# Stick-breaking attention laid out with keys on the partitions and its running sums on TensorE, a one-pass mask and maximum in the softmax blocks, and later output weight parts

## The reference, cut to what matters

```python
# dilated mixture: 12 heads, softmax over banded keys, q,k: 64 columns
s = where(valid, q @ k.T * Dh ** -0.5, -inf); m = max(s); p = exp(s - m); den = sum(p)
o = (p / den) @ v;  lse = m + log(den)          # heads are mixed by softmax(lse)

# latent attention: 8 heads, causal softmax, q,k: 96 columns
o = softmax(where(k <= q, s, -inf)) @ v

# stick breaking: 8 heads, q,k: 64 columns
z = q @ k.T * scale;  strict = k < q
log_one_minus = where(strict, log_sigmoid(-z), 0)
after = cumsum(log_one_minus, reverse) - log_one_minus     # sum over the later keys
weights = exp(where(strict, log_sigmoid(z) + after, -inf));  o = weights @ v

merged = gates[0] * (o_a @ wb_a) + gates[1] * (o_b @ wb_b) + gates[2] * (o_c @ wb_c)
x = x + merged @ w_out
```

## Time and profile before

| | |
|---|---|
| median of 3 runs | 5031.83 us (5019.65 to 5035.23) |
| the profiled execution | 5035.78 us, its span 5034.0 us |
| mean granted clock of TensorE | 0.941 of full speed |
| busy | PE 89%, PEld 62%, DVE 44%, ACT 30%, POOL 16% |
| stage C of the first layer | about 3236.6 to 3396 us in the span |
| the same of the second layer | about 4366.3 to 4525.7 us |

### The profile page before, as it was taken

The page is one execution under the profiler, slowest core; times in us unless marked ns, Lnnn a source line. Parts: engine busy times, 40 slices in busy tenths (PEclk is TensorE's granted clock), DMA queues, the critical chain, the costliest instruction groups (busy, mean ns, idle before and its releaser), DMA issues.

```text
span 5034.0 us, 90473 instructions
## 1 busy us (share of the span) xinstructions
PE 4482.8 (89%) x38676; PEld 3131.1 (62%) x38676; DVE 2228.4 (44%) x3897; ACT 1502.9 (30%) x2632; POOL 791.7 (16%) x499
## 2 busy tenths in 40 slices
PE   6899899988998899979998988878999988878999
PEld 3566666666555554464443965656787955656787
DVE  2555555453355542130112457446434357446343
ACT  2343333332222211010001334443332234443232
POOL 0021111110232230000000321233000321233000
PEclk9899999988999999989999999989999998989999
DMA  6100000000111024238998211114221211114221
GB/s 231 64 33 16 8 19 17 5 26 13 42 46 38 34 90 183 99 121 357 407 409 355 91 61 41 66 52 160 101 96 76 81 61 41 69 53 155 101 101 51
DMA packets 86825, 512.06 MB, mean 102 GB/s; under 512 B 10504, under 2 KB 11032, under 8 KB 45848
## 3 DMA queue, kind: packets, MB, share of 16 engines
q1 hardware_dynamic: 86424, 506.28, 26.3%
HBM read 476.85 MB, written 29.38 MB: 101 GB/s over the span
## 4 chain that ended last, share of the span: by engine, by line
PE 71%; DVE 13%; issue 7%; ACT 3%; DMA 3%; PEld 1%; POOL 1%; SPq 0%; PEldq 0%; DVEq 0%; POOLq 0%; ACTq 0%
PE ps L229 68%; PE ps L232 3%; DVE upper L248 2%; DVE upper L240 2%; ACT upper L287 2%; DMA upper<-in_ew 2%; DVE lower L240 2%; DVE upper L264 2%; PEld ps L229 1%; DVE upper L244 1%; DVE upper L256 1%; DVE rounded L240 1%; ACT lower L287 1%; DVE upper L260 0%; POOL upper L3702 0%
## 5 line engine op out<-in xcount | busy, mean ns | idle before, releaser
L229 PE MATMUL ps<-rounded,rounded 128*128 128x512 f32 (+2 forms) x7968 | 1672.4, 369 | 45.9 <-POOL rounded L3237 21.6
L229 PEld LDWEIGHTS ps<-rounded,rounded 128*128 128x128 f32 x7968 | 1345.9, 194 | 307.5 <-issue 36.0
L229 PE MATMUL ps<-lower 128*128 128x512 f32 (+10 forms) x4976 | 1078.0, 393 | 55.4 <-issue 22.8
L229 PE MATMUL ps<-upper 64*64 64x64 f32 (+8 forms) x15584 | 840.6, 260 | 173.0 <-DVE upper L264 38.9
L287 ACT ACTIVATE upper<-ps 128x512 f32<-128x512 f32 (+6 forms) x953 | 440.2, 491 | 1649.7 <-PE ps L229 1229.0
L229 PEld LDWEIGHTS ps<-upper 64*64 64x64 f32 (+4 forms) x15584 | 598.7, 145 | 445.7 <-issue 185.5
L229 PEld LDWEIGHTS ps<-lower 128*128 128x128 f32 (+3 forms) x4976 | 578.1, 184 | 442.9 <-issue 376.9
L229 PE MATMUL ps<-lower,upper 64*64 64x64 f32 (+6 forms) x7248 | 607.8, 304 | 52.1 <-DMA lower<-in_ada 21.3
L2616 POOL TENSOR_TENSOR rounded<-lower,rounded 128x1024 fp32r<-128x1024 f32 (+2 forms) x90 | 273.0, 3035 | 2009.3 <-ACT rounded L287 2009.0
L287 ACT ACTIVATE upper<-upper 128x512 f32<-128x512 f32 (+9 forms) x693 | 342.7, 501 | 648.7 <-DVE upper L260 167.9
L229 PEld LDWEIGHTS ps<-lower,upper 64*64 64x64 f32 (+3 forms) x7248 | 335.0, 143 | 263.1 <-issue 195.1
(11 more groups left out here) (89 smaller groups left out, 2444.5 us busy)
## 6 DMA issues: line engine op xcount, KB each, us to landing
lower<-in_ew SPq DMA_DIRECT2D x140, 1024.0 KB, 10.4
upper<-in_ew SPq DMA_DIRECT2D x52, 1024.0 KB, 12.9
lower<-in_b0f SPq DMA_DIRECT2D x16, 2048.0 KB, 7.5
lower<-in_b1f SPq DMA_DIRECT2D x16, 2048.0 KB, 7.8
upper<-in_ada SPq DMA_DIRECT2D x18, 1024.0 KB, 5.2
lower<-in_wrkv SPq DMA_DIRECT2D x8, 1728.0 KB, 7.1
lower<-in_b0g SPq DMA_DIRECT2D x24, 512.0 KB, 3.8
gad<-upper SPq DMA_DIRECT2D x48, 256.0 KB, 3.7
```

What stands on the lines that cost most here:

```text
L229: return self.e.matmul(out, lhsT, rhs, start=start, stop=stop)
```

## The change

**Softmax.** `stt` and `red` are replaced by one `tensor_tensor_reduce`, which adds the mask to the scores in PSUM, multiplies by minus the scale and keeps the minimum, so that the mask is scaled too; ACT's exp has scale -1. The built program holds two instructions for it. The score bank is free after it. The 48 negations of `softA` become one of 128x48 at meet latent.

**Stick breaking.** A step of the list is now a head, not a head and 128 queries. The scores stand transposed: keys on partitions, one block of columns for each of the 4 key blocks (512, 384, 128 and 256 queries; 1280 columns over three banks). The 1/8 is applied when the queries are copied out of PSUM. The mask is added by a matmul of the identity with a 128x128 constant. The sum over later keys is a matmul: a triangle of -1 for the key block itself, all -1 for later ones, against the value split into a rounded and a remaining part, accumulated in banks of its own head after the scores were copied out. No transposes, no scan and no POOL step remain. Two heads are in flight, three turns apart, and the filler comes at 1.78 steps a turn for 27 turns.

**Output weight parts.** They are made at d = 5, 6 and 7 and after the last.

```diff
+    def low(self, line, out, a, b, scale, least, *event):
+        self.wait_ge(line)
+        self.e.tensor_tensor_reduce(out, a, b, scale, 3e38, ADD, ALU.min, least).then_inc(line.up(*event), 1)
...
+    def heads(z):
+        for _ in range(3 * z):
+            yield None
+        for hh in range(z, 8, 2):
+            for s in (0, None, None, 1, None, 2):
+                yield None if s is None else ("stick", hh, s)
...
-    drain([lane("stick", 32, 5, z) for z in range(6)], filler, 1.4)
+    drain([heads(z) for z in range(2)], filler, 1.78)
...
+BLOCK_AT = (0, 512, 1024, 896)
...
+    def stick(hh, s):
+        team, slot, use = k.lane[hh % 2], hh % 2, ("stick", l, hh)
+        e = slice(64 * slot, 64 * slot + 64)
+        if s == 0:
+            ps = banks.take_at(use, 3 * slot, 3)
+            for j in (0, 1, 3, 2):
+                pe.mm(ps[:, block_cut(j)], b.ck[e, hh // 2, 128 * j:128 * j + 128], b.cq[e, hh // 2, 128 * j:512], j != 3, False)
+                last = pe.mm(ps[:, BLOCK_AT[j]:BLOCK_AT[j] + 128], pe.ident, k.c2["sb"], False, j != 1)
+            last.then_inc(team.pe.up("score", l, hh), 1)
+            return
+        ps = k.pair(use)
+        if s == 1:
+            pe.wait_ge(M.act, "sums", l)
+            pe.wait_ge(team.dve, "parts", l, hh)
+            pe.wait_ge(team.act, "kept", l, hh)
+            for j in (3, 2, 1, 0):
+                for i in range(j, 4):
+                    for part in (b.lost[slot], b.rest[slot]):
+                        last = pe.mm(ps[:, block_cut(j, i)], b.sums[:, 128:256] if i > j else b.sums[:, 0:128],
...
+        else:
+            pe.wait_ge(team.act, "exp", l, hh)
...
-            v.stt(t, o.p, k.pair(("score", *o.u))[:, 0:o.nk], o.scale, o.mask, MUL, ADD, "score", *o.u)
-            v.red(t, o.neg, o.p, MAX, "max", *o.u, negate=True)
+            v.low(t, o.p, k.pair(("score", *o.u))[:, 0:o.nk], o.mask, -o.scale, o.neg, "max", *o.u)
...
-                v.ts(t, b.mx[:, o.q:o.q + 1], o.neg, -1.0, MUL, event=("mx", *o.u))
...
+            v.wait_ge(team.act, "log", l, hh)
+            v.stt(t, b.raw[slot], ps[:, 0:1280], 0.0, b.soft[slot], MAX, ADD)
+            v.copy(t, b.lost[slot], b.raw[slot])
+            v.tt(t, b.rest[slot], b.raw[slot], b.lost[slot].bitcast(F32), SUB, "parts", l, hh)
+        elif s == 1:
+            v.wait_ge(team.pe, "less", l, hh)
+            v.tt(t, b.chance[slot], b.chance[slot], ps[:, 0:1280], ADD, "less", l, hh)
+        else:
+            v.wait_ge(team.pe, "value", l, hh)
+            v.copy(t, b.otC[:, :, 64 * hh:64 * hh + 64], v3(ps[:, 1280:1536], 64), "value", l, hh)
...
+            a.wait_ge(team.pe, "score", l, hh)
+            a.act(t, p, ps[:, 0:1280], AF.Abs)
+            a.copy(t, b.chance[slot], ps[:, 0:1280], "kept", l, hh)
+            a.act(t, p, p, AF.Exp, scale=-1.0)
+            a.act(t, p, p, AF.Ln, "log", l, hh, bias=1.0)
+        elif s == 1:
+            a.wait_ge(team.dve, "less", l, hh)
+            a.act(t, b.chance[slot], b.chance[slot], AF.Exp, "exp", l, hh)
...
-        if 0 < d < 5:
-            out_scalar(k, a, l, (d - 1) // 2, (d - 1) % 2)
+        if d > 4:
+            out_scalar(k, a, l, (d - 5) // 2, (d - 5) % 2)
     high(7)
+    out_scalar(k, a, l, 1, 1)
```

More of the change, by code:

```diff
@@ L307, in take, with take_at @@
         self.i = i + n if i + n < self.hi else self.lo
+        for b in range(i, i + n):
+            assert self.free.get(b, ()) is not None, "no bank is free"
+            if self.free.get(b):
+                self.pe.wait_ge(*self.free[b])
+            self.free[b] = None
+        self.pe.k.bank[use] = (i, n)
+        return self.pe.k.ps[:, 512 * i:512 * (i + n)]
+    def take_at(self, use, i, n):
         for b in range(i, i + n):
@@ L2538, in block2_map @@
     b.cq, b.ck, b.cv = v3(RB[:, 0:2048], 512), v3(RD[:, 0:2048], 512), v3(RC[:, 0:2048], 512)
-    b.on = RC[:, 2048:2560]
-    b.trip = [RA[:, 1536 * z:1536 * z + 1536] for z in range(6)]
+    at = ROUNDED + 4096
+    b.soft = [k.plain(at + 3840 * z, 1280) for z in range(2)]
+    b.chance = [k.plain(47272 + 1280 * z, 1280) for z in range(2)]
+    b.lost = [k.rounded(at + 3840 * z + 1280, 1280) for z in range(2)]
+    b.raw = [k.plain(at + 3840 * z + 2560, 1280) for z in range(2)]
+    b.rest = [k.rounded(at + 3840 * z + 2560, 1280) for z in range(2)]
+    b.sums = k.rounded(at + 7680, 256)
     up = ROUNDED + 4808
@@ L3032, in attend @@
             pe.mm(ps[:, 0:o.nk], o.query, o.key, True, True).then_inc(L.pe.up(*use), 1)
-            banks.give(use, L.dve, "score", *o.u)
-        elif s == (3 if stick else 2):
+            banks.give(use, L.dve, "max", *o.u)
+        elif s == 2:
             use = ("turn", *o.u)
@@ L3051, in attend @@
             banks.give(use, L.dve, *use)
+    def stick(hh, s):
[17 more added lines that the diff above has]
+                        last = pe.mm(ps[:, block_cut(j, i)], b.sums[:, 128:256] if i > j else b.sums[:, 0:128],
+                                     part[:, block_cut(i)], j != 1 and i == j and part is b.lost[slot],
+                                     j != 3 and i == 3 and part is b.rest[slot])
+            last.then_inc(team.pe.up("less", l, hh), 1)
+        else:
+            pe.wait_ge(team.act, "exp", l, hh)
+            for i in range(4):
+                for j in range(i + 1):
+                    p = b.chance[slot][:, BLOCK_AT[j] + 128 * (i - j):BLOCK_AT[j] + 128 * (i - j) + 128]
+                    for half in (slice(0, 64), slice(64, 128)):
+                        last = pe.mm(ps[half, 1280 + 64 * i:1344 + 64 * i], p[:, half], b.cv[:, j, 64 * hh:64 * hh + 64],
+                                     j == 0, j == i)
+            last.then_inc(team.pe.up("value", l, hh), 1)
+            banks.give(use, team.dve, "value", l, hh)
     for name, *z in b.order:
@@ L3289, in soft, with stick @@
                 v.ts(t, o.out, ps, o.den, MUL, event=("value", *o.u))
[L3291 to L3308 removed]
+    def stick(hh, s):
+        team, slot = k.lane[hh % 2], hh % 2
+        t, ps = team.dve, k.pair(("stick", l, hh))
+        if s == 0:
+            v.wait_ge(team.act, "log", l, hh)
[5 more added lines that the diff above has]
+            v.tt(t, b.chance[slot], b.chance[slot], ps[:, 0:1280], ADD, "less", l, hh)
+        else:
+            v.wait_ge(team.pe, "value", l, hh)
+            v.copy(t, b.otC[:, :, 64 * hh:64 * hh + 64], v3(ps[:, 1280:1536], 64), "value", l, hh)
     def mix(s):
@@ L3397, in block2_vector @@
         elif name == "meet":
+            if z == ["latent"]:
+                for lane in k.lane:
+                    v.wait_ge(lane.dve)
+                v.ts(tail.dve, b.mx, b.nm[:, 0:48], -1.0, MUL)
             v.meet("dve", (z[0], l))
```

95 lines of the change are left out of this document (28 added, 67 removed).

## The result

The changed kernel takes **5069.4 us** (median of 4 runs, 5065.4 to 5072.3) where the kernel before takes 5033.5 on the same chip: a ratio of 1.0076, interval 1.0056 to 1.0097. It is 36 us slower; 35 us faster was forecast. Two of the three parts of the change gave what was forecast or more. The third, the new stick-breaking, lost all of that and 36 us besides.

The account below looks back on a forecast made before the run. TensorE bounds only the second softmax stage; the others wait on DVE, POOL or chain length. Per layer 8 + 2 + 3 + 5 - 0.2 = 18 us, two layers 36: 5035.8 to 5000, 4996 beside the median; range 4958 to 5024.

Parts of the forecast that it names:

- One-pass mask and maximum: Softmax blocks: the fused instruction saves 8 us a layer in the first softmax stage and 2 in the second.
- I take 8: First softmax stage: us saved a layer, out of 11.3 us of DVE work saved; bounds 0 and 12.
- the 78 us that I looked at: 3010 to 3088 us in the first softmax stage, where DVE is busy 69.9 us and taken as the limit.
- hidden: Rest of the first softmax stage: DVE busy 48.8 of 106.5 us, less than half, its work taken as covered.
- Later output parts: Merge: without output parts d = 1 to 5 run at TensorE's pace; 5 us less a layer, bounds 2 and 12.
- Stage C: Stick-breaking stage: 156.5 us for 159.4, 3 us less a layer, between 20 less and 12 more.
- the walk: Stick-breaking heads laid out in order: third head starts at 30 us, three two-head rounds to 142, then 12.7: 155.
- the period: Stick-breaking: two heads repeat every 37.4 us, a path of 36.4 and 1.0 of wait; TensorE works 31.9.
- The filler on this path is four turns of 1.78 steps: Stick-breaking: filler on the path of two heads, put at 10.1 us of its 36.4.
- 1.5 us together: Stick-breaking: allowance for POOL holding rounding and remainder and for the clock falling after waits, taking 155 to 156.5.
- Rival (3): Stick-breaking chain with falling clock and POOL hold: period 45, stage 180 us, whole kernel 5044 beside the median; chance 0.09.
- Rival (1): Stick-breaking bound by work if scores near 2.3, rounding 0.8, clock up: stage 139 to 142 us, whole 4960; chance 0.25.

Follow-up runs that it names:

- Order: Changed kernel, odd head's sums issued before the even head's scores in the three turns where they stand together: 5035.5 us, ratio 1.0015.
- filler: Changed kernel with stick-breaking filler drawn at 2.22 a turn instead of 1.78: 5026.6 us, ratio 0.9992.
- hold: Changed kernel with GpSimd's stick-breaking remainders replaced by a second rounded copy on ScalarE (last four branches' gates wrong): 5032.5 us, ratio 1.0012.
- masks: Changed kernel with mask matmuls on rounded operands instead of float32: 5049.0 us, ratio 1.0041.
- the split of the sums: Kernel with sums first and filler at 2.22, the sums' matmuls of the rounded value issued before those of the rest: 4994.5 us, ratio 0.9929.
- parts' place: Kernel with sums first, filler at 2.22, split sums and rounded masks; stick-breaking weight parts issued just ahead of a head's scores: 4966.0 us, ratio 0.9869.
- last parts: The kernel of parts' place with three more weight parts moved, two ahead of the first head's scores, one ahead of the last's: 4953.1 us, ratio 0.9857.
- the repaired kernel: Changed kernel with sums first, filler at 2.22, split sums, rounded masks: 4973.7 us; with weight parts also moved (stage 142.8 us): 4953.1.
- both moves: Weight parts issued ahead of heads' scores, then three more moved, on the kernel with sums first, 2.22, split, rounded masks: ratio 0.9889 to 0.9857.

## Why the prediction was wrong

- **One-pass mask and maximum.** Direction right, size too small: 41 us for 20. VectorE is busy 89.7 us in stage A. The term that was mis-sized is "I take 8", bounds 0 and 12: stage A gave 17.8. Reading the accumulator takes 0.083 us where 0.154 was taken, 1.7 us over the 24. The starts of the scores, which come in the same order in both traces, tell where the 17.8 arose: 4.4 us ahead of the 78 us that I looked at, 10.5 in them and 2.9 behind. So the 8 was 2.5 too small for its own stretch, and 7.3 us came from the rest of the stage, whose VectorE work I had called hidden. The advice quoted from the Trainium skill (VectorE: DVE Perf Modes, section Rules for kernel authors), by which this would give nothing, does not hold here: the pair took 0.68 and 0.69 us at 512 columns, the fused form 0.69 and 0.083.
- **Later output parts.** Right: 5 us a layer forecast, 5.5 by the trace, and 10 for both layers by the run alone. TensorE waits for VectorE's held operations at d = 6 and 7 alone, 11.1 us ahead of `oproj`.
- **Stage C.** This is the step that failed: 156.5 us forecast, 203 measured. By the walk's own marks: start of the third head's scores 42.5 us after the first's (30 forecast), then two heads in 42.6, 45.3 and 44.2 (37.4), then 28 us (12.7). The places and the releasers of the waits in the period were right. In the period of 45.3 us the step from an even head's scores to the values of the odd head before it took 19.5 us for 16.15, and the scores alone, at the lower clock, took 3.6 more (7.4 for 3.8); the step from these values to the next even head's scores took 25.75 us for 21.2, of which 2.3 more are the wait (3.3 for 1.0). What was wrong are four sizes, and one idea.
  - Scores with masks take 4.4 us at full clock, not 3.8: from start to start the four score blocks take 2.9 us where 2.55 was read, and the four masks 1.5 where 1.3 was, both read from rows of other shapes (without masks between them the same blocks take 2.35). That is 5 us a layer.
  - "The filler on this path is four turns of 1.78 steps" counts too much. The list from which 1.78 a turn is drawn also holds the 12 weight parts, so a turn brings 1.42 filler steps (48/60 of 1.78). The waits were less filled, and 11 steps, 15.7 us, came after the last head. Drawing at 2.22 is worth 42 us in the whole.
  - GpSimd's hold was foreseen ("will at times hold the rounding and the remainder") but stands in the walk at nothing and behind it inside "1.5 us together". It met five of the eight rounding copies: where nothing held them, VectorE's three operations took 3.8 us for the 4.45 of the walk, and in the odd heads 5.6. In the first head VectorE's three operations took 7.4 us for the 4.45 of the walk; of the 12.5 us by which the third head started late these are 3, and 6.8 more are the first sums (5.35 for 2.8) and the second scores (8.1 for 3.8) at the lower clock.
  - "1.5 us together" for hold and clock. This was the error that weighed most. The kernel with no GpSimd work in the stage does its 890 matmuls in 137.8 us at a clock of 1.00; the changed kernel takes 167.5 for 892, the same work in another order. So some 30 us of the 203 are the price of the lower clock, and 36 are idle. The 66 us of work that stand at the lower level, which would take half at full clock, say the same: 33.
  - The idea: costs were added as if each stood alone. Order, filler, hold and masks were worth 31, 42, 32 and 18 us each on the changed kernel, 123 in sum, and the split of the sums 25 more on its own base. In a row (order, filler, split, masks, parts' place, last parts) they gave 31, 18, 25, 20, 10 and 6: 110. The parts act on each other, and both ways. The filler found less left behind the new order, 18 us for 42. GpSimd's work cost more there: taking it away is worth 32 us on the changed kernel and 71 behind order and filler, since in that order it holds all eight copies; and without it order and filler together are worth 88 us (1.0012 to 0.9837), with it 49.
- **Rival (3)** named the mechanism, chain and falling clock with GpSimd's hold, and its place, period 45 and stage 180. The periods measured are 42.6 to 45.3; what it lacks of 203 is the start and the tail. It was given 0.09 on the ground that before's waits are longer and more in number. That ground does not hold: before has 40.5 us idle in stage C at a clock of 0.87, the changed kernel 35.8 at 0.82. How often a wait is followed by work at the lower clock was not read from the trace, though the earlier trace rows shows it: 8 transposes take 2.32 us right behind the wait of 6.82. In the trace of before the lower level lasts for 41.0 us of stage C, in that of the changed kernel for 71.7.
- **Rival (1)**, bound by work, is what the repaired kernel does: 142.8 us, against 139 to 142. That the numbers agree is in part luck: of its three conditions only the rounding at 0.8 us came true; scores with rounded masks take 3.9 us, not 2.3, and the clock was 0.93.

What stays open: filling the list to its end won 42 us, 21 a layer, more than the 15.7 of the tail. In the trace of the first layer the stage is 12.1 us shorter in waits and 7.8 in the same matmuls, at a clock of 0.86 for 0.82; which waits the steps filled was not followed. No kernel was run that keeps the waits and holds the clock by other work, which would price the clock alone.

## What to carry to other kernels

When a change turns many short units into a few long chains, walk the chain with the durations at the lower clock wherever the walk itself predicts a wait, and price the stage both ways; waits of 3.3 to 4.7 us were here mostly followed by matmuls at nearly twice their price. Before a rounding copy or a subtraction goes on VectorE's critical chain, look at what GpSimd does in that stretch, and try to issue GpSimd's work when VectorE waits for ScalarE. On the repaired kernel this gave 16 us with both moves, on the changed one nothing clear of the error, because there TensorE came to wait for the remainders. And when a number sets how filler is drawn, count what the list holds, not what it is named for.

## What was not expected of the hardware

- A VectorE copy that rounds float32 to the rounded form, SBUF to SBUF, takes 0.83 us for 1280 columns, and waits as a whole for a GpSimd subtraction: 2.4 to 2.6 us beside one of 2.4 us. With GpSimd idle its mean over eight was 0.828. The Trainium skill (SBUF — State Buffer, section SBUF: two separate sides) says that VectorE in a mode that uses two ports, or with two SBUF inputs while the GpSimd operation reads SBUF, and GpSimd lock each other out for a whole instruction; the trace agrees on VectorE's side, the copy with one input included. Operations with an input from PSUM were never held: in the whole trace of the changed kernel over 50 additions of 128x512 with one such input began inside a GpSimd subtraction, and all took 0.69 us, as elsewhere.
- VectorE's add with minimum over a PSUM and an SBUF input is a custom instruction and costs no more than the plain mask operation: 0.69 us at 512 columns, 0.083 for the accumulator.
- A float32 matmul of 128x128 by an identity holds TensorE for 0.42 us at full clock (0.72 at half), the rounded one, between float32 scores, still for 0.26. Rounded ones among themselves took 0.15 each on average, though they are of 128 to 512 columns (3.0 us for the 20 of the sums).
